# Giving up TensorE's products of constants behind the norms and around the routing positions

## The chip, the cores and the metric

The kernel runs on one core of one Trainium2 chip. The metric is device time in microseconds (us) of one execution. A core has a matrix engine (TensorE, PE in the rows; PEld is its weight load), VectorE (DVE), ScalarE (ACT), GpSimd (POOL) and SyncE (SP), which issues most DMAs. The engines run side by side and meet at semaphores; each works through its own instructions in program order.

## The reference, cut to what matters

Two layers of a transformer, for 128 context tokens (group 0) and 128 latent tokens (group 1), 1024 features, all in float32. Per layer an attention sub-layer, then a mixture of 16 experts, each behind a post-norm:

```
for l in range(2):
    hp, hs = modulate(xp, mp[0], mp[1]), modulate(xs, ms[0], ms[1])   # x * (1 + scale) + shift
    op, os_ = attention of the layer (hp / hs, caches)                # l = 0: MLA + windowed GQA, l = 1: GQA
    xp = layer_norm(ALPHA * xp + mp[2] * op, ...)                     # xs likewise
    hp, hs = modulate(xp, mp[3], mp[4]), ...
    fp, fs = moe(hp, ...), moe(hs, ...)
    xp = layer_norm(ALPHA * xp + mp[5] * fp, ...)                     # xs likewise

def moe(h, ...):
    aff = sigmoid(x @ router_w); sel = aff + router_bias              # best group of 4, best 2 experts in it
    ...
    hid = silu(x @ w_gate[e]) * (x @ w_up[e])
    y   = sum over experts of (hid * gate[e]) @ w_down[e]
```

The experts' weights are 192 MB for the two layers; with the other weights the core moves 287 MB.

## The kernel before, in words

All weights come through a ring of ten blocks of 2 MB. SP issues the loads in one fixed order; a load waits until TensorE has released the block that it overwrites. So loading runs ahead of TensorE by at most ten blocks, and stops when the ring is full.

Each engine's program is written out by hand. TensorE's runs, per layer: `modulated(l, 0)` (the normalised tokens are transposed, four 128x128 products per half of the features and group), the input projection (`project` or `project_odd`), `attention`, `ln_rows`, `modulated(l, 1)`, `route`, `experts`, `ln_rows`. In the experts the tokens are gathered by one-hot products into 64 slots per expert (`gather`), and a pair of experts takes 6 ring blocks: 4 for gate and up (`gate_up`, L1094), 2 for down (`down`, L1128). The first block of a pair is released at the fifth of the eight feature steps of `gate_up`.

A seam here is the stretch between two dense pieces of TensorE's work in which it waits for other engines. There are three kinds around the change. Letters name them below:

- Seam A, layer 0, from the attention's output projection to the experts. VectorE adds the sub-layer to x and computes the norm, group 0 first (`add_up`, `normal`, L1519), with a power on GpSimd between (L1985). TensorE transposes each group when its normalised rows are there (L739); ScalarE and VectorE copy the transposes out, modulated (L1771, L1322). Then come the router's logits (L1038, 16 columns each), `turn_back` (16 transposes of the modulated tokens, L753, copied out by ScalarE, L1757), and `route`: VectorE chooses the experts in a chain of small operations up to L1611, TensorE counts positions with products of `tri` and `ones` (L1051 to L1057), VectorE makes the first one-hots from them (L1618, L1623), and TensorE gathers (L1065). The gathered tokens are copied out by ScalarE (L1855), and `gate_up` starts.
- Seam B, from layer 0's experts to layer 1's input projection (`project_odd`, L789): norm, transposes, projection.
- Seam C, layer 1, from its attention to its experts: as A, but group 0 has been transposed and its logits computed inside the attention, so only group 1 is left.

The function `keep_busy(key, n)` (L716 to L720) issues n products of two constants, 128x128 by 128x512 in float32, into the bank that the work behind it will overwrite. A float32 product stands as two records in the trace. It is called in `modulated` before the wait for each group's normalised rows (3 then 2 products in seams A and B, 3 in C), in `route` before the wait for the chosen experts (3), and at the end of `route`, ahead of the gathers (1). No result of it is used.

Of the kernel before, what the change touches and what calls it, by code (L numbers as in the profile page):

```python
# [55 lines left out]
HALF = 512  # L56
# [247 lines left out]
def hybrid_backbone(nc, i_, o_):  # L304
# [11 lines left out]
    with ExitStack() as ctx:  # L316
        def sb(name, cols, dt=F32):
            return ctx.enter_context(nc.sbuf_tensor(name, [P, cols], dt))
# [8 lines left out]
        const = sb("const", C_COLS)  # L327
# [91 lines left out]
        def cst(c, n, rows_=P):  # L419
            return const[0:rows_, c:c + n]  # L420

        ident = cst(C_ID, P)
# [3 lines left out]
        def ar(off, n):  # L426
            return arena[:, off:off + n]

        hT = ar(0, G * D).rearrange("p (g k t) -> p g k t", g=G, k=KD)
# [75 lines left out]
        def room(eng, key, e=None):  # L505

            b, t = turn[key]
            if e is not None:
                eng.wait_ge(drained[b], e + t)
            elif t > 0:  # L510
                eng.wait_ge(drained[b], t)
# [5 lines left out]
        def fill(key):  # L517
            return filled[turn[key][0]], 1
# [4 lines left out]
        def pb(key):  # L523
            return bank[turn[key][0]]
# [142 lines left out]
        def _(pe):  # L667
# [45 lines left out]

                turn_rows(("modT", l, s), mods[l], C_SEL + 12 * s, 8)

            def keep_busy(key, n):  # L716

                room(pe, key)
                for _ in range(n):
                    nc.tensor.matmul(pb(key)[:], ident, const[:, 0:HALF], start=True, stop=True, skip_group_check=True)  # L720

            def modulated(l, s):

                for g in range(1 if (l, s) == (1, 1) else 0, G):
                    if (l, s) == (0, 0):
                        pe.wait_ge(s_x, 32)
                    else:
                        keep_busy(("hT", l, s, g, 0), 3 if (l, s) == (1, 1) else 3 - g)
                        pe.wait_ge(s_xn, G * (2 * l + s - 1) + g + 1)
                    for q in range(2):  # L730
                        rows_turned(l, s, g, q)

            def rows_turned(l, s, g, q):

                src = x if (l, s) == (0, 0) else xn_odd if (l, s) == (1, 1) else xn
                key = ("hT", l, s, g, q)
                room(pe, key)
                for k in range(4):
                    mm = nc.tensor.transpose(pb(key)[:, k * P:(k + 1) * P],  # L739
                                             src[:, g, (4 * q + k) * P:(4 * q + k + 1) * P], ident)  # L740
                    if (l, s, g, q, k) == (1, 1, 1, 0, 0):
                        mm.then_inc(*release(index[("wout", 1, 1)]))
                mm.then_inc(*fill(key))

            def turn_back(l):

                for g in range(G):
                    for q in range(2):
                        key = ("hr", l, g, q)
                        room(pe, key)  # L750
                        pe.wait_ge(*saved(("hT", l, 1, g, q)))
                        for k in range(4):
                            mm = nc.tensor.transpose(pb(key)[:, k * P:(k + 1) * P], hT[:, g, 4 * q + k, :], ident)  # L753
                        mm.then_inc(*fill(key))
# [276 lines left out]
            def logits(l, g):  # L1031
                key = ("logits", l)
                if g == 0:
                    room(pe, key)
                pe.wait_ge(*saved(("hT", l, 1, g, 0)))
                pe.wait_ge(*saved(("hT", l, 1, g, 1)))
                for k in range(KD):
                    mm = nc.tensor.matmul(pb(key)[:, g * N_EXP:(g + 1) * N_EXP], hT[:, g, k, :], rw[:, k, :],  # L1038
                                          start=(g == 0 and k == 0), stop=(k == KD - 1), skip_group_check=True)
                if g == 1:  # L1040
                    mm.then_inc(*fill(key))

            def route(l):
                for g in range(l, G):
                    logits(l, g)
                turn_back(l)
                key = ("pos", l)
                keep_busy(key, 3)
                pe.wait_ge(s_ch, l + 1)
                out = pb(key)  # L1050
                nc.tensor.matmul(out[:, 0:32], tri, chosen[:], start=True, stop=False, skip_group_check=True)  # L1051
                nc.tensor.matmul(out[:, 16:32], ones, chosen[:, 0:16], start=False, stop=True,
                                 skip_group_check=True).then_inc(*fill(key))
                room(pe, ("all", l))
                everyone = pb(("all", l))[:, 64:80]
                nc.tensor.matmul(everyone, ones, chosen[:, 0:16], start=True, stop=False, skip_group_check=True)
                nc.tensor.matmul(everyone, ones, chosen[:, 16:32], start=False, stop=True,  # L1057
                                 skip_group_check=True).then_inc(*fill(("all", l)))
                keep_busy(("xe", l, 0), 1)

            def gather(out, onehot, chunks, width):

# [200 lines left out]
            for l in range(DEPTH):  # L1263
                if l == 0:
                    pe.wait_ge(s_rows, 48)
                    pe.wait_ge(s_const, 16)
                    turn_rows(("lnT",), rows, C_ID + LN_ROW, 16)
                    pe.wait_ge(s_cwin, 1)
                    modulation(0, 0)
                    pe.wait_ge(*saved(("mod", 0, 0)))  # L1270
                    mod_columns(0, 0)
                modulated(l, 0)
                if l == 0:
                    project(0)
                    modulation(0, 1, (index[("win", 0, len(WIN[0]) - 1)],))
                else:
                    project_odd()
                attention(l)
                ln_rows(l, 0)
                modulated(l, 1)  # L1280
                if l == 0:
                    pe.wait_ge(s_load, SMALL_LOADS)
                route(l)
                experts(l)
                overflow(l)
                ln_rows(l, 1)
# [815 lines left out]
```

## Time and profile before

| | before |
|---|---|
| time, median of 3 runs | 830.72 us (828.36 to 832.08) |
| the profiled execution's own time | 832.93 us |
| its span, first to last instruction | 831.0 us |
| mean granted TensorE clock | 0.972 of full speed |
| PE busy | 760.6 us, 92% |
| DMA | 287.46 MB, mean 346 GB/s |
| products of constants (L720) | 21, in 42 records |

The span is 1.9 us shorter than the execution's own time; those 1.9 us lie before the first and after the last instruction. PE busy counts an instruction from its start to its modelled end, and consecutive ones overlap, so the start-to-start distance tells more than the mean duration. The granted clock is given as a share of 2.4 GHz: 1.00 is 2.4 GHz, 0.50 is 1.2 GHz. DMA runs at about 418 GB/s when nothing holds it back, and stands still in the seams because the ring is full.

### The profile page before, as it was taken

Reading aid. Unit: us, or ns where it says so; the run is one execution under the profiler, and the core shown is the slowest. Engines: PE = TensorE matmul, PEld = TensorE weight load, DVE = VectorE, ACT = ScalarE, POOL = GpSimd, SP = SyncE. Lnnn points to the kernel's source line nnn. Section 1 sums busy time; section 2 is a strip of 40 time slices with the busy share of each in tenths; the row PEclk is TensorE's granted clock in tenths of the full one; section 3 lists DMA queues with packets and bytes.
Section 4 is the critical chain, followed back from the end, with each engine's and each line's share of the span. In section 5 each row is a group of like instructions: output and inputs, shape, how many; then the busy total and the mean of one; then the engine's idle time right before and its main releaser. Section 6 shows DMA issues by size and latency. Waiting matters only on the chain.

```text
span 831.0 us, 9612 instructions
## 1 busy us (share of the span) xinstructions
PE 760.6 (92%) x3769; PEld 364.8 (44%) x3769; DVE 237.1 (29%) x550; ACT 150.9 (18%) x390; POOL 59.9 (7%) x116
## 2 busy tenths in 40 slices
PE   3798898999999999997899999999999999997794
PEld 1345344556544444343234564455544433443231
DVE  0004433348410101000237237475411010010056
ACT  0201212225011111111112132232211101110020
POOL 0000000000100010101000110000100001101000
PEclk9899799999999999999999999999899999999997
DMA  8999999915399999999999999752199999999971
GB/s 304 390 307 396 391 388 418 396 44 203 122 418 416 419 421 416 418 420 412 421 398 374 371 356 421 299 213 111 51 420 417 420 419 415 421 416 417 419 305 51
DMA packets 78530, 287.46 MB, mean 346 GB/s; under 512 B 6508, under 2 KB 12140, under 8 KB 62100
## 3 DMA queue, kind: packets, MB, share of 16 engines
q1 hardware_dynamic: 74452, 275.60, 83.8%
q10 hardware_dynamic: 2880, 7.03, 2.1%
q0 software_dynamic: 1152, 4.19, 1.3%
q8 instruction: 32, 0.52, 0.3%
q14 instruction: 14, 0.11, 0.0%
HBM read 278.99 MB, written 7.82 MB: 345 GB/s over the span
## 4 chain that ended last, share of the span: by engine, by line
PE 51%; SPq 29%; DMA 8%; DVE 7%; ACT 2%; issue 2%; POOL 0%; DVEq 0%; ACTq 0%
PE bank L1094 14%; SPq L600 12%; PE bank L1128 7%; SPq L595 6%; PE bank L932 5%; DMA ring<-in_exp_w_up 5%; PE bank L789 5%; SPq L596 4%; PE bank L1065 3%; DMA ring<-in_w_mod 3%; SPq L572 3%; PE bank L671 3%; PE bank L878 2%; PE bank L820 2%; ACT arena L1801 2%
## 5 line engine op out<-in xcount | busy, mean ns | idle before, releaser
L1094 PE MATMUL bank<-ring,arena 128*64 128x512 f32 x1024 | 228.5, 601 | 16.4 <-DMA ring<-in_exp_w_up 15.6
L1094 PEld LDWEIGHTS bank<-ring,arena 128*64 128x64 f32 x1024 | 75.5, 138 | 165.8 <-issue 151.5
L1128 PE MATMUL bank<-ring,arena 128*64 128x512 f32 x512 | 113.8, 595 | 5.9 <-DMA ring<-in_exp_w_down 4.9
L1678 DVE TENSOR_TENSOR arena<-bank,arena 128x256 f32<-128x256 f32 x32 | 13.6, 425 | 233.7 <-ACT arena L1847 233.7
L1128 PEld LDWEIGHTS bank<-ring,arena 128*64 128x64 f32 x512 | 36.5, 137 | 71.5 <-issue 64.3
L1065 PE MATMUL bank<-arena 128*128 128x128 f32 x512 | 62.1, 275 | 0.0
L1065 PEld LDWEIGHTS bank<-arena 128*128 128x128 f32 x512 | 59.7, 192 | 1.0 <-DVE arena L1623 0.5
L1757 ACT ACTIVATE arena<-bank 128x512 f32<-128x512 f32 (+6 forms) x67 | 37.2, 579 | 107.3 <-PE bank L789 34.0
L1847 ACT ACTIVATE arena<-bank 128x256 f32<-128x256 f32 x32 | 12.3, 384 | 227.5 <-PE bank L1094 227.5
L1694 DVE COPY arena<-bank 128x512 f32<-128x512 f32 x14 | 9.7, 691 | 118.7 <-PE bank L1128 118.7
L789 PE MATMUL bank<-ring,arena 128*128 128x256 f32 (+1 forms) x128 | 41.6, 486 | 0.0
L2004 POOL TENSOR_SCALAR arena<-const,cur 128x64 f32<-128x64 f32 x56 | 24.1, 446 | 213.3 <-PE bank L1073 210.5
L1985 POOL TENSOR_TENSOR rstd<-ss,mhalf 128x1 f32<-128x1 f32 (+2 forms) x11 | 12.6, 1142 | 360.0 <-DVE ss L1514 246.7
L820 PE MATMUL bank<-ring,cwin 128*32 128x512 f32 x256 | 32.7, 652 | 2.6 <-DMA ring<-in_w_mod 2.6
L1801 ACT ACTIVATE arena<-bank,negm 128x128 f32<-128x128 f32 (+1 forms) x64 | 26.1, 417 | 36.1 <-DVE negm L1440 36.1
L769 PE MATMUL bank<-ring,arena 128*128 128x416 f32 (+2 forms) x96 | 32.1, 495 | 0.7 <-ACT arena L1771 0.7
L789 PEld LDWEIGHTS bank<-ring,arena 128*128 128x128 f32 x128 | 24.2, 190 | 16.9 <-issue 15.3
L1859 ACT ACTIVATE arena<-bank 128x512 f32<-128x512 f32 x18 | 10.8, 597 | 108.8 <-PE bank L1128 108.8
L932 PE MATMUL bank<-ring 128*128 128x512 f32 x64 | 29.8, 599 | 0.0
L932 PE MATMUL bank<-ring,arena 128*128 128x512 f32 x64 | 29.8, 598 | 0.0
L1431 DVE TENSOR_REDUCE mx<-bank 128x2 f32<-128x512 f32 (+1 forms) x24 | 16.5, 689 | 44.0 <-PE bank L878 44.0
L692 PE MATMUL bank<-ring,cwin 128*32 128x512 f32 x128 | 18.1, 708 | 12.0 <-DMA ring<-in_w_mod 12.0
(182 smaller groups left out, 683.8 us busy)
## 6 DMA issues: line engine op xcount, KB each, us to landing
ring<-in_exp_w_gate SPq DMA_DIRECT2D x64, 1024.0 KB, 19.6
ring<-in_exp_w_up SPq DMA_DIRECT2D x64, 1024.0 KB, 20.1
ring<-in_exp_w_down SPq DMA_DIRECT2D x64, 1024.0 KB, 23.6
ring<-in_w_mod SPq DMA_DIRECT2D x24, 2048.0 KB, 19.8
expert_rows<-arena ACTq DMA_DIRECT2D x12, 512.0 KB, 7.9
ring<-in_w_out_ab SPq DMA_DIRECT2D x2, 2048.0 KB, 19.9
ring<-in_w_in_c SPq DMA_DIRECT2D x2, 2048.0 KB, 22.9
ring<-in_w_out_c SPq DMA_DIRECT2D x2, 2048.0 KB, 12.8
```

What stands on the lines that cost most here:

```text
L595: sp.dma_start(dst[:, 0], w_gate[e + t // 2, :, half]).then_inc(got(n + t)[0], 16)
L596: sp.dma_start(dst[:, 1], w_up[e + t // 2, :, half]).then_inc(got(n + t)[0], 16)
L600: sp.dma_start(dst[:, a].rearrange("p (k c) -> p k c", k=2), w_down[e + a, :, half]).then_inc(got(n + t)[0], 16)
L769: mm = nc.tensor.matmul(pb(key)[:, 0:c1 - c0], hT[:, g, k, :], w[:, k, :], start=(k == 0), stop=(k == KD - 1))
L789: mm = nc.tensor.matmul(pb(key)[:, 0:c1 - c0], hT[:, g, k, :], w[:, k, :], start=(k == 0), stop=(k == KD - 1))
L820: mm = nc.tensor.matmul(out[32 * j:32 * j + 32, :], cwin[:, k, 24 - 2 * c:56 - 2 * c], w[:, k * HALF:(k + 1) * HALF], start=(c == first an ...
L932: mm = nc.tensor.matmul(pb(key)[:], out_T(l, u)[:, ci * P:(ci + 1) * P], w[:, (c % 4) * D + hf * HALF:(c % 4) * D + (hf + 1) * HALF], star ...
L1065: mm = nc.tensor.matmul(out[:, i * width:(i + 1) * width], hr[:, g, k * P:(k + 1) * P], onehot[:, g, 0:width], start=(g == 0), stop=(g == 1))
L1094: mm = nc.tensor.matmul(pb(key)[SLOTS * hf:SLOTS * (hf + 1), :], xeT[b][:, k * P + SLOTS * a:k * P + SLOTS * (a + 1)], w[:, :, k % 4, hf * ...
L1128: mm = nc.tensor.matmul(pb(key)[SLOTS * a:SLOTS * (a + 1), :], hp[:, c:c + SLOTS], w[:, a, kf % 2, hf * HALF:(hf + 1) * HALF], start=(kf = ...
L1757: A.activation(dst, pb(key)[:] if src is None else src, ACT.Copy).then_inc(*drain(key))
L1801: ins = A.activation(prob[b][:, i * nk:(i + 1) * nk], pb(("S", l, u))[:, i * nk:(i + 1) * nk], ACT.Exp, bias=negm[b][:, i:i + 1], scale=sc ...
```

## The change

The function `keep_busy` and its four calls go. Where the call in `route` also made the bank's wait (`room`), that wait stays in its place. Nothing else moves.

```diff
-            def keep_busy(key, n):
-
-                room(pe, key)
-                for _ in range(n):
-                    nc.tensor.matmul(pb(key)[:], ident, const[:, 0:HALF], start=True, stop=True, skip_group_check=True)
-
             def modulated(l, s):
 
                 for g in range(1 if (l, s) == (1, 1) else 0, G):
                     if (l, s) == (0, 0):
                         pe.wait_ge(s_x, 32)
                     else:
-                        keep_busy(("hT", l, s, g, 0), 3 if (l, s) == (1, 1) else 3 - g)
                         pe.wait_ge(s_xn, G * (2 * l + s - 1) + g + 1)
                     for q in range(2):
                         rows_turned(l, s, g, q)
@@
                 turn_back(l)
                 key = ("pos", l)
-                keep_busy(key, 3)
+                room(pe, key)
                 pe.wait_ge(s_ch, l + 1)
                 out = pb(key)
                 nc.tensor.matmul(out[:, 0:32], tri, chosen[:], start=True, stop=False, skip_group_check=True)
@@
                 nc.tensor.matmul(everyone, ones, chosen[:, 16:32], start=False, stop=True,
                                  skip_group_check=True).then_inc(*fill(("all", l)))
-                keep_busy(("xe", l, 0), 1)
```

TensorE's program in seam A before the change, from the end of the rows of the norm's weights (L671) to the logits (L1038). An `x` behind a row is the number of such instructions in a row, a bracket what the first waits for:

```order
L671 MATMUL bank<-rows,const 128x512 [waits drained5]
L720 MATMUL bank<-const 128x512 [waits drained0]
L720 MATMUL bank<-const 128x512 x2
L739 MATMUL bank<-const,arena 128x128 [waits drained0,normalised_x_ready]
L739 MATMUL bank<-const,arena 128x128 x3
L739 MATMUL bank<-const,arena 128x128 [waits drained1]
L739 MATMUL bank<-const,arena 128x128 x3
L720 MATMUL bank<-const 128x512 [waits drained2]
L720 MATMUL bank<-const 128x512
L739 MATMUL bank<-const,arena 128x128 [waits drained2,normalised_x_ready]
```

The same place in the changed kernel, whose lines have other numbers (L739 is L732):

```order
L671 MATMUL bank<-rows,const 128x512 [waits drained5]
L732 MATMUL bank<-const,arena 128x128 [waits drained0,normalised_x_ready]
L732 MATMUL bank<-const,arena 128x128 x3
L732 MATMUL bank<-const,arena 128x128 [waits drained1]
L732 MATMUL bank<-const,arena 128x128 x3
L732 MATMUL bank<-const,arena 128x128 [waits drained2,normalised_x_ready]
```

Each group's transposes now stand directly behind the work before them, with only their wait between.

TensorE's program at the end of `route` before the change, from the last transposes of `turn_back` (L753) over the positions to the first gather (L1065):

```order
L753 MATMUL bank<-const,arena 128x128 [waits drained3,drained1]
L753 MATMUL bank<-const,arena 128x128 x3
L720 MATMUL bank<-const 128x512 [waits drained7]
L720 MATMUL bank<-const 128x512 x2
L1051 MATMUL bank<-chosen,const 128x32 [waits experts_chosen]
L1052 MATMUL bank<-chosen,const 128x16
L1056 MATMUL bank<-chosen,const 128x16 [waits drained7]
L1057 MATMUL bank<-chosen,const 128x16
L720 MATMUL bank<-const 128x512 [waits drained0]
L1065 MATMUL bank<-arena 128x128 [waits drained3,drained1,drained2,drained0,onehot_ready]
```

The same place in the changed kernel:

```order
L746 MATMUL bank<-const,arena 128x128 [waits drained3,drained1]
L746 MATMUL bank<-const,arena 128x128 x3
L1044 MATMUL bank<-chosen,const 128x32 [waits experts_chosen,drained7]
L1045 MATMUL bank<-chosen,const 128x16
L1049 MATMUL bank<-chosen,const 128x16 [waits drained7]
L1050 MATMUL bank<-chosen,const 128x16
L1057 MATMUL bank<-arena 128x128 [waits drained3,drained1,drained2,drained0,onehot_ready]
```

The positions' products now wait for the chosen experts right behind `turn_back`, and the gather for the one-hots right behind the positions. No other engine's program changes.

## Rows read from the trace of the kernel before

**Rows 1.** The page's 40 slices of the span: GB/s moved.

```profile
GB/s 304 390 307 396 391 388 418 396 44 203 122 418 416 419 421 416 418 420 412 421 398 374 371 356 421 299 213 111 51 420 417 420 419 415 421 416 417 419 305 51
```

**Rows 2.** The chain that ended last: start, duration, what.

```profile
295.49 1.30 SPq L600
...
447.77 37.83 PE bank L789 x112
```

**Rows 3.** SP's first DMA issues behind seams A and C: start, duration, count.

```profile
220.74 4.31 SPq L600 DMA_DIRECT2D ring<-in_exp_w_down  x4
...
599.30 4.32 SPq L600 DMA_DIRECT2D ring<-in_exp_w_down  x4
```

**Rows 4.** TensorE in seam A, in order of time.

```profile
193.53 2.74 PE L720 MATMUL bank<-const 128*128 128x512 f32 x6
196.10 1.04 PE L739 MATMUL bank<-const,arena 128*128 128x128 f32 x8
...
198.70 1.04 PE L739 MATMUL bank<-const,arena 128*128 128x128 f32 x8
199.88 3.72 PE L1038 MATMUL bank<-rw,arena 128*128 128x16 f32 x32
...
209.47 0.30 PE L1051 MATMUL bank<-chosen,const 128*128 128x32 f32 x2
...
211.75 3.73 PE L1065 MATMUL bank<-arena 128*128 128x128 f32 x32
```

**Rows 5.** VectorE in seam A: norms, chosen experts, first one-hots.

```profile
192.76 0.80 DVE L1519 TENSOR_SCALAR arena<-x,bnmv,rstd 128x1024 f32<-128x1024 f32 x1
...
196.71 0.81 DVE L1519 TENSOR_SCALAR arena<-x,bnmv,rstd 128x1024 f32<-128x1024 f32 x1 [0.67 <-POOL rstd L1985]
...
207.14 0.19 DVE L1611 SCALAR_TENSOR_TENSOR chosen<-chosen,gsel 128x32 f32<-128x32 f32 x1
...
210.32 0.74 DVE L1623 TENSOR_SCALAR arena<-const,pg 128x64 f32<-128x64 f32 x4
```

**Rows 6.** TensorE in seam B.

```profile
441.05 2.74 PE L720 MATMUL bank<-const 128*128 128x512 f32 x6
...
446.67 1.09 PE L739 MATMUL bank<-const,arena 128*128 128x128 f32 x8 [0.29 <-DVE arena L1519]
```

**Rows 7.** TensorE in seam C.

```profile
576.00 1.04 PE L739 MATMUL bank<-const,arena 128*128 128x128 f32 x8
578.59 2.64 PE L1038 MATMUL bank<-rw,arena 128*128 128x16 f32 x16 [1.55 <-DVE arena L1322]
581.07 3.65 PE L753 MATMUL bank<-const,arena 128*128 128x128 f32 x16
...
588.05 0.30 PE L1051 MATMUL bank<-chosen,const 128*128 128x32 f32 x2
...
590.32 3.73 PE L1065 MATMUL bank<-arena 128*128 128x128 f32 x32
```

**Rows 8.** VectorE in seam C: norm of group 1, chosen experts.

```profile
574.68 0.81 DVE L1519 TENSOR_SCALAR arena<-x,bnmv,rstd 128x1024 f32<-128x1024 f32 x1 [0.68 <-POOL rstd L1985]
...
584.71 0.19 DVE L1611 SCALAR_TENSOR_TENSOR chosen<-chosen,gsel 128x32 f32<-128x32 f32 x1
```

**Rows 9.** Stretches: us, busy PE PEld DVE ACT POOL, PEclk, DMA share, GB/s.

```profile
204.20:207.60 3.40, 3.40 (x13) 2.71 (x12) 3.00 (x16) 3.40 (x4) 0.00 (x0) 0.51 0.00 0
81.20:94.60 13.40, 10.36 (x52) 4.27 (x50) 4.24 (x13) 3.80 (x19) 0.00 (x0) 0.50 1.06 389
750.30:753.70 3.40, 3.40 (x16) 0.86 (x12) 0.00 (x0) 0.00 (x0) 0.46 (x1) 1.00 1.03 430
757.30:760.70 3.40, 3.40 (x10) 1.21 (x8) 0.00 (x0) 0.00 (x0) 0.77 (x1) 0.53 1.00 408
579.60:586.30 6.70, 6.70 (x28) 5.67 (x28) 4.92 (x20) 3.90 (x5) 0.00 (x0) 0.50 0.49 208
753.90:757.30 3.40, 1.32 (x6) 0.58 (x8) 0.85 (x2) 0.23 (x1) 2.48 (x4) 0.97 1.02 424
```

## The prediction

> **What bounds the kernel now.** I read the page's slices first. GB/s stands near 418 through both expert stretches and falls to 44, 203, 122 around seam A and to 299, 213, 111, 51 around seam C, so loading stops in the seams [rows 1]. Then the chain of waits: at 295.49 it passes to SP's issues, that is to the loads, and at 447.77 it is TensorE itself that is bound, for 37.8 us of layer 1's projection [rows 2]. Then SP's issues: behind seam A the first comes at 220.74, when the first pair of experts has released a block; behind seam C at 599.30 [rows 3]. So the experts of a layer end at a fixed distance behind the first release, and whatever moves `gate_up`'s start moves the end by as much. In seam B nothing but TensorE's own start of the projection counts. The order of TensorE, VectorE and ScalarE in each seam tells what moves that start. Last the granted clock by stretches.
>
> **What goes.** 21 products, 0.86 us each (3 products, 6 records, take 196.10 - 193.53 = 2.57 us) [rows 4]. Their 18 us of issue don't count as such: only where one is still running when the work behind it could start.
>
> **Seam A, the order alone.** Group 0's normalised rows are ready at 192.76 + 0.80 = 193.56; its transposes start at 196.10. That alone gains nothing, since group 1 is normalised only at 196.71 + 0.81 = 197.52. Group 1's transposes start at 198.70: they can start 1.15 us earlier, and with them the logits, because ScalarE's copies of group 0, 2.5 us earlier too, are no longer what they wait for. The chosen experts are ready at 207.14 + 0.19 = 207.33, but TensorE works off three products of constants and starts the positions at 209.47: 2.1 us in the way [rows 4, 5]. The one-hots are ready at 210.32 + 0.74 = 211.06, the gather starts at 211.75 behind the last product: 0.65 us [rows 4, 5]. Together 1.15 + 2.1 + 0.65 = 3.9 us at full clock.
>
> **Seam C, the order alone.** Group 1 is ready at 574.68 + 0.81 = 575.49, transposed from 576.00: 0.5. Chosen at 584.71 + 0.19 = 584.90, positions from 588.05: 3.15. One-hots to gather as in A: 0.65. Together 4.3 us [rows 7, 8].
>
> **Seam B, the order alone.** Group 1's transposes start at 446.67 and already waited 0.29 us for VectorE [rows 6]; the projection stands behind them. Nothing is gained.
>
> **What the clock takes.** The trace shows two levels. TensorE was granted 1.2 GHz from 204.2 to 207.6, although it had been busy all of the time before, with 32 logits of 16 columns each from 199.88 to 203.6 [rows 4, 9]. It was granted 1.2 GHz from 579.6 to 586.3 (a wait of 1.55 us and again logits ahead of it), from 757.3 to 760.7 (idle 2.1 of the 3.4 us ahead), and for 13.4 us from 81.2 [rows 7, 9]. At 1.2 GHz gate and up starts 10 products in 3.4 us where it starts 16 at 2.4 GHz [rows 9]; 16 transposes take 3.65 us, where 8 take 1.04 [rows 7]; a logit takes 0.165 us instead of 0.116 (3.72/32; in seam C 16 of them took 2.64, of which some 5 at full clock) [rows 4, 7]. So a 3.4 us stretch of dense work at half clock costs 1.3 to 1.7 us.
>
> The changed kernel leaves TensorE idle where products of constants stood, so I expect the fall earlier and also later than now:
>
> - A, before the logits: behind 193.6 there are 1.0 us of transposes, 2.9 us of nothing, 1.0 us of transposes, then logits. That is thinner than what stood ahead of the falls at 204.2 and 757.3, so I expect 1.2 GHz by about 198.5. Transposes at half cost 0.7, the 32 logits 1.6; between 0 and 2.3, I take 1.9. The chosen experts then come at 207.33 - 1.15 + 1.9 = 208.1, positions at once instead of at 209.47 (1.4 earlier), gather at 208.1 + 1.6 (209.47 to 211.06, as now) + 0.15 for small products at half clock = 209.85: 1.9 earlier than 211.75.
> - A, gather and first pair: all of `turn_back` is dense and may bring the clock back, but 2 us of nearly nothing follow while VectorE makes positions and one-hots. A gather at half clock takes some 7.1 us instead of 3.6. Between 0 and 3.4, one long stretch wholly at half clock; nearest are the rows of 3.4 us at half clock, 1.3 to 1.7, and I take 1.4 since part of that stretch may be over by then. Net for A: -1.9 + 1.4 = -0.5. Ends: -3.9 and +1.9.
> - B: behind 441.05 there is idle time until group 0 is ready, 1.0 us of transposes, and 2.9 us of idle up to 446.67. That is as thin as the time ahead of 757.3 [rows 6, 9], so I expect the projection to begin at 1.2 GHz. It is bound by TensorE [rows 2], so all of it counts: between 0 (the clock holds) and 3.4 (twice the 3.4 us at half), I take the single stretch, 1.5. No other work hides it.
> - C: logits and `turn_back` already ran at half clock [rows 9]; the fall a little earlier costs about 0.6 more, so chosen experts at 585.0, positions at once, gather at 586.7 instead of 590.32: 3.6 earlier. In the kernel before, the three products behind `turn_back` ran while the clock came back; now gather and `gate_up` do. Between 0 and 3.4, again 1.4. Net -2.2. Ends: -4.3 and 0.
>
> Sum: -0.5 + 1.5 - 2.2 = -1.2 us. Against the profiled execution's own 832.93 (span 831.0 and 1.9 around it) that is 831.7; that execution lies 2.2 above the median of the runs, so against 830.72 it is **829.5 us**. From the ends: -8.2 and +5.3, that is 822.5 and 836.0. The forecast is therefore no difference that can be told: a measurement of this kernel tells about 0.5%, 4.2 us.
>
> Half-clock stretches inside the expert stretches behind the first releases cost nothing before and after, since DMA sets the pace there (757.3 to 760.7 moved 408 GB/s [rows 9]). They may move about.
>
> **The rivals.**
>
> *The clock is back before both gathers.* `turn_back`'s 16 transposes may restore it and the short lull not take it. For it: at 586.3 it returned after transposes and products. Against it: the lull behind. Then A gives 1.9, C 3.6, B costs 1.5: -4.0, 826.7.
>
> *The clock never falls more than before.* Nothing but the order counts: -8.2, 822.5. Against it: the clock fell at 204.2 and 579.6 even with the products of constants, and the thin stretches are now longer [rows 9].
>
> *The clock stays at half through the dense work as well: slower.* One mechanism, in all three seams: the fall is not undone by the first dense stretch but only by a second one, as in the 13.4 us from 81.2, where TensorE was busy 10.4 us and still at 1.2 GHz [rows 9]. Then gather with `gate_up` pays 3.4 twice and the projection 3.4, and A's logits their 2.3: A +1.9, B +3.4, C 0: +5.3, 836.0. It decides when the half-clock stretches over dense work sum to more than 16 us over the three seams, against the 8.2 of gain. Against it: at 760.7 the clock was back after one stretch of gate and up [rows 9].
>
> The Trainium skill's page "TensorE: Matmul & The Clock Gate", section "HAM oscillation — how this bites in real kernels", tells of a kernel in which every group of products behind a wait for DMA starts throttled, and advises to order the work so that TensorE stays warm; by that account each of the three seams pays a throttled start, which is the forecast's time or this rival's. The trace agrees at 757.3, behind a wait for DMA, where the clock is 0.53 of 2.4 GHz [rows 9].
>
> *It doesn't matter at all*, because something else restarts the loads: 830.7. Against it: the loads move 44 GB/s in the slice from 187 us and resume with SP's issue at 220.74 [rows 1, 3].
>
> **How the numbers follow.** Forecast (-1.2, own range 826.5 to 832.5) 0.56; clock back before the gathers 0.15; clock never falls further 0.07; clock stays at half 0.13; no effect 0.09. Faster than 826.6: all of 822.5's case, nearly half of 826.7's, a little of the forecast: 0.17. Slower than 834.9: somewhat over half of the slow case and a little of the forecast: 0.10. Same: 0.73. The range that leaves out 2 in 10 runs from 825.5 to 834.0.
>
> **What would show it.** In seam A, positions start 0.05 to 0.1 us behind the chosen experts, and the gather as close behind the one-hots; logits at 0.165 us each with the clock at 0.50. Gather starts near 209.9 and 586.7 on the old scale. In B the projection begins at the same distance behind the norm, with clock 0.50 for about 3.4 us. SP's first issue of w_down in each layer moves by A's and C's net. I am wrong if the gathers run at half clock for their whole length in both layers and `gate_up` too (slower), or if the clock at all three seams is full (faster).

## The result and the profile after

| | before | after |
|---|---|---|
| time, median | 828.82 us (826.94 to 832.08, 9 runs) | 833.75 us (831.2 to 837.15, 9 runs) |
| ratio | | 1.0051 (95% interval 1.003 to 1.0071) |
| profiled execution, own time and span | 832.93, 831.0 us | 833.75, 831.9 us |
| mean granted clock in it | 0.972 | 0.967 |
| PE busy | 760.6 us | 752.8 us |

The change makes the kernel slower by 0.5%, some 4.2 us (2.5 to 5.9). The differences in us given here and below are worked out from the recorded ratio and its interval; the plain difference of the two medians is 4.9. The forecast was 1.2 us faster. Already here something asks for care: the profiled executions differ by 0.8 us only. The profile before came from an execution slower than the nine timed ones of the table. Two single executions of later runs, one without seam B's products and one with narrow products, took 1467 and 1580 us and stand in no ratio.

Where each profiled execution spent its time can be read from five distances on TensorE: from the start of the norm's weight rows (L671, eight records) of layer 0 to the first gate and up (A), on to the same rows behind layer 0's experts, from there to those of layer 1 (B, with the whole attention), on to layer 1's first gate and up (C), and on to the end.

| us | A | experts 0 | B | C | to the end |
|---|---|---|---|---|---|
| before | 26.21 | 221.40 | 132.37 | 24.80 | 236.21 |
| after | 27.49 | 221.34 | 133.70 | 23.50 | 236.50 |
| difference | +1.28 | -0.06 | +1.33 | -1.30 | +0.29 |

The sum of the differences is +1.5; the stretch up to seam A was 0.6 shorter, though nothing in it is changed, which leaves the span's +0.9. The two expert stretches differ by no more than 0.3 us between the executions, so what a seam gains or loses does reach the end in full, as the prediction had it.

TensorE in seam A after (start, duration, line, operands, count, and the wait in brackets):

```profile
189.37 3.68 PE L671 MATMUL bank<-rows,const 128*128 128x512 f32 x8
192.98 1.09 PE L732 MATMUL bank<-const,arena 128*128 128x128 f32 x8
196.94 1.55 PE L732 MATMUL bank<-const,arena 128*128 128x128 f32 x8 [2.87 <-DVE arena L1511]
198.28 6.85 PE L1031 MATMUL bank<-rw,arena 128*128 128x16 f32 x32
204.97 3.24 PE L746 MATMUL bank<-const,arena 128*128 128x128 f32 x16
208.95 0.38 PE L1044 MATMUL bank<-chosen,const 128*128 128x32 f32 x2 [0.73 <-DVE chosen L1603]
...
210.66 5.46 PE L1057 MATMUL bank<-arena 128*128 128x128 f32 x32 [0.16 <-DVE arena L1615]
...
216.86 7.52 PE L1086 MATMUL bank<-ring,arena 128*64 128x512 f32 x34
```

The queue is gone as expected: group 1's transposes follow the norm, the positions stand 0.15 us behind the chosen experts (208.80) and the gather 0.05 us behind the one-hots, where there were 2.1 and 0.65 us [rows 4, 5]. The logits are counted here by their records, two to a product, as the prediction counts them: seam A's 32 are 16 products. These 32 take 6.85 us instead of 3.72 and the gather 5.46 instead of 3.73 [rows 4]. The stretches of that execution say why (us; busy PE, PEld, DVE, ACT, POOL; granted clock; DMA share; GB/s):

```profile
197.20:207.60 10.40, 10.40 (x53) 10.40 (x52) 6.16 (x20) 3.21 (x7) 0.00 (x0) 0.51 0.37 156
...
211.20:214.20 3.00, 3.00 (x16) 3.00 (x16) 2.86 (x7) 0.07 (x1) 2.09 (x6) 0.50 0.00 0
446.80:450.00 3.20, 2.74 (x10) 2.23 (x11) 1.14 (x4) 1.66 (x5) 0.00 (x0) 0.50 1.06 388
580.00:586.60 6.60, 6.50 (x31) 6.53 (x32) 5.15 (x18) 2.16 (x4) 0.00 (x0) 0.50 0.66 277
590.00:593.20 3.20, 3.20 (x18) 3.20 (x17) 3.09 (x8) 0.60 (x1) 2.56 (x8) 0.50 0.00 0
```

In seam A TensorE is at 1.2 GHz from 197.2 to 207.6, over the second transposes, all logits and nearly all of `turn_back`, comes back to 2.4 GHz for the lull, and falls again in the gather. Before, it was at half clock from 204.2 to 207.6 alone [rows 9]. In seam C it is at half clock over the logits (3.57 us for 16) and again in the gather. Seam B, which was at full clock before, has the projection's start at half:

```profile
443.29 1.09 PE L732 MATMUL bank<-const,arena 128*128 128x128 f32 x8 [1.49 <-DVE arena L1511]
447.26 1.97 PE L732 MATMUL bank<-const,arena 128*128 128x128 f32 x8 [2.88 <-DVE arena L1511]
449.02 7.53 PE L782 MATMUL bank<-ring,arena 128*128 128x512 f32 x16
```

Behind the second group's norm the eight transposes take 1.97 us instead of 1.09 [rows 6], then the projection follows; nothing starts earlier in return. Seam C after, in order of time:

```profile
571.90 3.60 PE L671 MATMUL bank<-rows,const 128*128 128x512 f32 x8
577.46 1.09 PE L732 MATMUL bank<-const,arena 128*128 128x128 f32 x8 [1.96 <-DVE arena L1511]
580.11 3.57 PE L1031 MATMUL bank<-rw,arena 128*128 128x16 f32 x16 [1.55 <-DVE arena L1314]
583.51 3.41 PE L746 MATMUL bank<-const,arena 128*128 128x128 f32 x16
587.49 0.38 PE L1044 MATMUL bank<-chosen,const 128*128 128x32 f32 x2 [0.56 <-DVE chosen L1603]
...
589.20 5.47 PE L1057 MATMUL bank<-arena 128*128 128x128 f32 x32 [0.16 <-DVE arena L1615]
```

The gather starts 17.30 us behind the weight rows instead of 20.33, and its slower run gives 1.7 of these 3.0 us back. SP's first issue of w_down follows in both layers; in layer 0 it is at

```profile
221.39 3.80 SPq L600 DMA_DIRECT2D ring<-in_exp_w_down  x3
```

0.65 us later than in [rows 3], as A's gate and up is (216.86 against 216.22).

### The profile page after: what moved, and what is told of

It is laid out like the page before. It is cut to its first block, busy times and chain, and to the rows that moved or that the text cites. A ratio compares the mean times of both kernels' runs of the same rounds, so it can differ in the third digit from the quotient of the medians.

```text
span 831.9 us, 9530 instructions
## 1 busy us (share of the span) xinstructions
PE 752.8 (90%) x3727; PEld 365.6 (44%) x3727; DVE 237.3 (29%) x550; ACT 151.0 (18%) x390; POOL 59.9 (7%) x116
## 4 chain that ended last, share of the span: by engine, by line
PE 48%; SPq 29%; DVE 10%; DMA 8%; issue 2%; ACT 2%; POOL 0%; DVEq 0%
PE bank L1086 14%; SPq L600 12%; PE bank L1120 7%; SPq L595 6%; DMA ring<-in_exp_w_up 5%; PE bank L782 5%; PE bank L925 5%; PE bank L1057 4%; SPq L596 4%; DMA ring<-in_w_mod 3%; SPq L572 3%; PE bank L871 2%; PE bank L813 2%; ACT arena L1793 2%; PE bank L1031 1%
## 5 line engine op out<-in xcount | busy, mean ns | idle before, releaser
L1057 PE MATMUL bank<-arena 128*128 128x128 f32 x512 | 65.5, 285 | 0.3 <-DVE arena L1615 0.3
L1057 PEld LDWEIGHTS bank<-arena 128*128 128x128 f32 x512 | 62.8, 201 | 0.5 <-DVE arena L1615 0.5
```

The lines of the kernel that those rows point to most:

```text
L1057: mm = nc.tensor.matmul(out[:, i * width:(i + 1) * width], hr[:, g, k * P:(k + 1) * P], onehot[:, g, 0:width], start=(g == 0), stop=(g == 1))
```

## The experiments

Theory 1: the products bought clock. The wide products behind the norms keep TensorE at 2.4 GHz over the logits and the projection, those in `route` over the gather, and the clock is worth more than the queue. Theory 2, the rival, takes different forms: the products act only by their place in the queue, or the loss comes from the gathers alone, or the difference lies outside the seams.

**The norms' products alone taken away.**

```diff
-                        keep_busy(("hT", l, s, g, 0), 3 if (l, s) == (1, 1) else 3 - g)
```

> The products of constants behind the norms go (seams A, B and C); those in route stay. Theory 1 (what the norms' products kept up is TensorE's clock over the router's logits and over layer 1's projection): seam A gains 1.15 us by the order and loses 3.1 on 32 logits at 0.21 us each instead of 0.116 and 0.5 on transposes, B loses 1.4, C about 0.7: +4 to +5 us against the kernel before, with the clock at 0.50 over the logits of layer 0. Theory 2 (the products only stand in the way, and the loss of the changed kernel comes from the gathers behind route): the norms' part alone gives -1 to -2 us.

Measured: 837.36 against 832.4 us, ratio 1.0047 (1.0029 to 1.0066), +3.9 us. Distances: A 28.04, B 134.03, C 24.33. As theory 1 had it, if just below its +4 to +5; theory 2's -1 to -2 is out. Against the 4.2 us of the whole change, nearly all of the loss is in this part.

**Route's products alone taken away.**

```diff
-                keep_busy(key, 3)
+                room(pe, key)
...
-                keep_busy(("xe", l, 0), 1)
```

> Only the products in route go (three ahead of the positions, one ahead of the gathers, in both layers); those behind the norms stay. Theory 1: the queue in front of the positions and gathers goes, 2.1 + 0.65 us in seam A and 3.15 + 0.65 in C, and about 1.5 to 1.7 us each is given back by a gather or first gate and up at half clock: -2 to -4 us against the kernel before. Theory 2 (the loss of the changed kernel comes from here): +3 us or more, with gather and gate and up at half clock in both layers.

Measured: 831.72 against 832.4 us, ratio 0.9992 (0.9971 to 1.0013). Neither: no difference that can be told, where theory 1 said -2 to -4 and theory 2 +3 (the interval is -2.4 to +1.1 us, so only theory 1's upper edge lies inside). The stretches at half clock in this execution:

```profile
202.60:212.80 10.20, 9.52 (x44) 9.04 (x45) 8.11 (x33) 3.88 (x5) 1.89 (x5) 0.50 0.00 0
585.00:591.90 6.90, 6.67 (x32) 6.68 (x33) 6.34 (x27) 0.60 (x1) 4.01 (x11) 0.52 0.00 0
```

In seam C the gather lies inside the second of them:

```profile
584.28 0.38 PE L1051 MATMUL bank<-chosen,const 128*128 128x32 f32 x2 [1.97 <-DVE chosen L1610]
...
586.10 6.46 PE L1064 MATMUL bank<-arena 128*128 128x128 f32 x32
```

TensorE waited 1.97 us for the chosen experts, at full clock until then; the clock fell at 585.0, and the gather took 6.46 us instead of 3.73 and the positions' products 0.6 us instead of 0.4. So the queue that is saved (gather 3.7 us earlier in C) comes back as clock to more than half: C is 23.80, A 26.10.

**Seam B's products alone taken away.**

```diff
-                        keep_busy(("hT", l, s, g, 0), 3 if (l, s) == (1, 1) else 3 - g)
+                        if (l, s) != (1, 0):
+                            keep_busy(("hT", l, s, g, 0), 3 if (l, s) == (1, 1) else 3 - g)
```

> Only the five products behind the norm ahead of layer 1's projection (seam B) go. Theory 1: nothing stands earlier, and the projection's first 3.4 us run at half clock, with eight transposes: +1.3 us or up to +2.6, clock 0.50 at the projection's start. Theory 2 (the projection has slack or the clock holds): 0.

Measured: ratio 1.0026 (1.0004 to 1.0047), +2.2 us; B is 135.12. The clock fell while TensorE was idle and did not return with the first dense work:

```profile
443.80:450.40 6.60, 5.41 (x13) 3.35 (x14) 4.18 (x8) 2.39 (x7) 0.28 (x1) 0.50 1.05 385
```

Theory 1, within its +1.3 to +2.6. This execution also had a seam A with the products kept in which the clock never fell: 25.02 us, against 26.21 in the profile before, with the same code. That was the first sign that one profile does not stand for the kernel.

**Seam A's norm products alone taken away**, by the same edit with `(0, 1)`.

> Only the five products behind the norm of seam A go. Theory 1: the transposes start 1.15 us earlier, 32 logits at 0.21 us instead of 0.116 cost up to 3.1 and the transposes 0.7 at most: seam A 1 to 2.5 us longer than before, the rest as before: +1 to +2.5 us. Theory 2 (the logits are paced by their weight loads and not by the clock): -1.15.

Measured: ratio 1.0044 (1.002 to 1.0069), +3.7 us; A is 29.43, B and C 132.41 and 24.79. The logits:

```profile
197.45 6.85 PE L1039 MATMUL bank<-rw,arena 128*128 128x16 f32 x32
204.14 3.65 PE L754 MATMUL bank<-const,arena 128*128 128x128 f32 x16
207.59 3.38 PE L720 MATMUL bank<-const 128*128 128x512 f32 x6
```

The loss is above theory 1's range, though its interval (1.7 to 5.7 us) reaches into it: the three products ahead of the positions still stand there, now behind a `turn_back` that is late itself. The form of theory 2 in which the logits are paced by weight loads whatever the clock is out: 0.21 us a record at half clock, 0.116 at full. The losses measured alone, 3.7 for A and 2.2 for B, sum to more than the 3.9 of all the norms' products together; the intervals (1.7 to 5.7, 0.3 to 3.9 and 2.4 to 5.5) leave room for that.

**Every product kept in place and length, but narrow.** Each product of 512 columns becomes four of 16:

```diff
-                for _ in range(n):
-                    nc.tensor.matmul(pb(key)[:], ident, const[:, 0:HALF], start=True, stop=True, skip_group_check=True)
+                for _ in range(4 * n):
+                    nc.tensor.matmul(pb(key)[:, 0:16], ident, const[:, 0:16], start=True, stop=True, skip_group_check=True)
```

> Every product of constants is kept in place and in length, but as four products of 16 columns instead of one of 512 (about 0.9 us, as a logit takes 0.116 us per record). So TensorE's order and its waits are those of the kernel before, and what it does in the seams is what the logits do. Theory 1 (the wide products buy clock, and wide columns are what buys it): it has both costs, the queue in the way and the half clock: +6 to +10 us against before, slower than the changed kernel. Theory 2 (the products act only by their place and time): like the kernel before, within 1 us.

Measured: ratio 1.0178 (1.0138 to 1.0217), +14.8 us. TensorE from the logits of seam A to the gather, with the three former products of 512 columns now as 24 records, and below it the clock:

```profile
203.64 3.65 PE L753 MATMUL bank<-const,arena 128*128 128x128 f32 x16
207.09 5.14 PE L720 MATMUL bank<-const 128*128 128x16 f32 x24
212.06 0.61 PE L1051 MATMUL bank<-chosen,const 128*128 128x32 f32 x2
...
216.01 5.42 PE L1065 MATMUL bank<-arena 128*128 128x128 f32 x32
```

```profile
202.30:219.40 17.10, 16.75 (x80) 16.64 (x80) 9.23 (x34) 3.89 (x5) 2.09 (x6) 0.50 0.01 1
```

TensorE is busy 16.75 of 17.10 us and at half clock throughout. This is the decisive run: same order, same waits, hardly any idle time, and A 32.65, B 135.29, C 28.21. So the rival that the products act only by their place and time is out: with the narrow products TensorE was occupied and the clock was at half, while with the wide ones in the same places none of the four profiled executions of the kernel before had more than 6.8 us at half clock in one seam. The loss is more than theory 1's 6 to 10 because the narrow products slow down themselves (24 in 5.14 us; the 24 ahead of seam A's transposes, at full clock, took 2.75). How the 14.8 us divide between the two was not measured.

**The changed kernel and the kernel before, profiled again.** Both unchanged.

> The changed kernel once more, for a second profiled execution: the first had seam A at 27.49 us from the norm's weight rows to the first gate and up, B at 133.70 to the same rows of layer 1, C at 23.50, where the kernel before had 26.21, 132.37 and 24.80. Theory 1 (the clock's falls decide, and where one falls shifts from execution to execution): the stretches outside the seams repeat within 0.2 us, A lies between 26 and 29, B between 133 and 135.5, C between 22.5 and 25, with the logits of A at half clock again. Theory 2 (each part's cost is fixed): all three repeat within 0.2 us.

> The kernel before once more, for a second profiled execution. Theory 1: A between 25.0 (no fall, as in the run without B's products) and 26.2, B 132.4, C 24.8. Theory 2: A 26.2 again.

> The kernel before, a third profiled execution, to see one with a mean clock of 0.975 or more. Its timed executions go with the mean clock: 826.4 to 828.1 us at 0.979 to 0.982, 832.6 to 835.4 at 0.967. Theory 1: if this one has a clock of 0.975 or more, seams A and C together are 3 to 6 us shorter than the 51.0 of the first two, since the clock does not fall over the logits or not for long; if it has 0.967, it repeats them. Theory 2: the difference lies outside the seams.

> The kernel before, a fourth profiled execution, with the same purpose and the same expectations as the third.

| execution | own time, us | mean clock | A | B | C |
|---|---|---|---|---|---|
| before, first | 832.93 | 0.972 | 26.21 | 132.37 | 24.80 |
| before, second | 832.6 | 0.967 | 27.86 | 132.41 | 23.13 |
| before, third | 826.65 | 0.979 | 25.03 | 132.42 | 21.98 |
| before, fourth | 827.99 | 0.979 | 25.03 | 132.41 | 21.98 |
| mean of before | | | 26.0 | 132.4 | 23.0 |
| after, first | 833.75 | 0.967 | 27.49 | 133.70 | 23.50 |
| after, second | 833.29 | 0.962 | 27.18 | 134.09 | 23.42 |
| mean of after | | | 27.3 | 133.9 | 23.5 |

The expectation for the second of before missed A (27.86, where 25.0 to 26.2 was said) and C (23.13 for 24.8); the clock was at half from 202.7 to 209.5 in its seam A and from 581.6 to 585.0 in its seam C. Otherwise theory 1, with two corrections. Seams A and C together are 47.0 us in the third and the fourth, 4.0 shorter than in the first two, as was expected; but of the 6.2 us between the spans of the first and the third another 2.3 lie ahead of seam A (its weight rows start at 190.01 and 187.72), so theory 2 holds for that part. And over all its timed executions the clock orders the time less sharply than was expected (numbers in the last section). The kernel before has executions with and without the falls. In the third TensorE stays at full clock over the logits of both layers:

```profile
197.58:203.43 5.85, 5.57 (x48) 5.33 (x49) 5.57 (x19) 3.06 (x7) 0.00 (x0) 1.00 0.30 125
575.19:579.25 4.06, 3.78 (x33) 3.54 (x33) 3.83 (x12) 1.81 (x3) 0.00 (x0) 1.00 0.99 414
```

and its seam C, in order of time, is 2.8 us shorter than that of the first execution [rows 7]:

```profile
575.19 1.93 PE L1038 MATMUL bank<-rw,arena 128*128 128x16 f32 x16 [1.55 <-DVE arena L1322]
576.96 1.51 PE L753 MATMUL bank<-const,arena 128*128 128x128 f32 x12
...
579.25 2.74 PE L720 MATMUL bank<-const 128*128 128x512 f32 x6
581.83 0.30 PE L1051 MATMUL bank<-chosen,const 128*128 128x32 f32 x2
...
588.57 3.65 PE L1094 MATMUL bank<-ring,arena 128*64 128x512 f32 x16 [0.73 <-issue]
```

With the products some executions keep the clock over the logits and some don't; in neither profile without them, nor in any of the nine timed executions of the changed kernel (mean clock 0.954 to 0.972, 831.2 us the fastest), was the clock as high as before's 0.979. By the means A costs 1.3, B 1.5 and C 0.5: +3.3 us, inside the interval of the timed +4.2. The means stand on four and two executions, which is few.

**One product ahead of the positions, none ahead of the gathers; the norms' products kept.**

```diff
-                keep_busy(key, 3)
+                keep_busy(key, 1)
...
-                keep_busy(("xe", l, 0), 1)
```

> Ahead of the positions one product instead of three in both layers, none ahead of the gathers; the norms' products stay. Theory 1: TensorE is free when the chosen experts come or 0.5 us later, instead of 2.1 and 3.15 us later; the one-hots lead to the gather 0.65 us earlier. Seam A 0.6 to 1.5 us shorter than before, C 1.5 to 3 shorter, less 0 to 1.7 each for a gather at half clock: -1 to -3 us in all, better than taking all of route's products away (-0.7). Theory 2 (any wide product there delays more than it saves): equal to or slower than with none of route's products, about 0.

> The same kernel as with one product ahead of the positions and none ahead of the gathers, timed again to narrow its interval (0.9977, 0.9951 to 1.0004 the first time). Theory 1: 0.996 to 0.999 again, -1 to -3 us, seam A 24 to 26 us and C 19 to 23.5. Theory 2 (the first result was chance): 1.000 or above.

Measured: ratio 0.9977 (0.9951 to 1.0004), then 0.9949 (0.9922 to 0.9976). The first of these alone settles nothing, the second is faster than before clear of its interval; the two overlap. A is 23.96 and 25.59, C 21.02 and 22.37. In the first, C runs at full clock all through, and is 1.0 us shorter than with three products in an execution without a fall either (21.98).

**Two products there in layer 1, one in layer 0.** `keep_busy(key, 1 + l)`, the rest as above.

> As the last, but two products ahead of the positions in layer 1, where TensorE waited 1.0 us for the chosen experts with one. Theory 1: where the logits of seam C ran at half clock the second product comes 0.9 us in the way, where they ran at full clock it fits into the wait: within 1 us of one product. Theory 2 (more products always keep more clock): 1 to 2 us faster than with one.

Measured: 826.93 against 832.43 us, ratio 0.9932 (0.9908 to 0.9956), 5.7 us faster than before and the fastest of all kernels run. Its seam A, from the product ahead of the positions:

```profile
204.69 1.02 PE L720 MATMUL bank<-const 128*128 128x512 f32 x2
206.36 0.41 PE L1051 MATMUL bank<-chosen,const 128*128 128x32 f32 x2 [0.65 <-DVE chosen L1610]
...
208.11 3.84 PE L1064 MATMUL bank<-arena 128*128 128x128 f32 x32 [0.16 <-DVE arena L1622]
...
212.68 7.52 PE L1093 MATMUL bank<-ring,arena 128*64 128x512 f32 x34
```

TensorE still waits 0.65 us for the chosen experts, and the gather takes 3.84 us, at full clock. The clock was at half over most of seam C's logits (C is 23.40) and back at full for the gather. Against one product the intervals overlap, so which of the two is better stays open. These runs change two things at once, the number ahead of the positions and the one product ahead of the gathers; what each is worth was not run.

## Why the prediction was wrong

- *What bounds the seams, and that they reach the end in full*: right. Each of the two expert stretches repeats within 0.5 us over all 14 profiled executions, while A runs from 23.7 to 32.7.
- *The order alone*: right. Positions behind the chosen experts by 0.15 us, gather behind the one-hots by 0.05, second transposes behind the norm: all queue that was named is gone.
- *Seam B*: right in size. 1.5 forecast; +1.3 in the first pair of profiles, +1.5 in the means, +2.2 us when timed alone.
- *The fall in A by about 198.5*: right, at 197.2. *What the logits pay for it*: the first step that failed, a mis-sized term. The price of a logit at half clock, 0.165 us, is 2.64/16, the mean over seam C's 16 logits, although some of them ran at full clock. The rows had the right price already: these logits start at 578.59, the clock fell at 579.6 and `turn_back` starts at 581.07 [rows 7, 9], so some nine of them ran at full clock, not five, and the other seven took 1.5 us. It is 0.21 (6.85/32, and 3.40 from start to start for 16 in C). The 32 of A lose 3.1 us, not 1.6. So the chosen experts of A came 2.1 us later, against 0.75 forecast, and the gather 0.45 earlier, against 1.9 (21.29 behind the weight rows, 21.74 before).
- *The gathers' half clock*: nearly right, 1.7 us in each layer (6.20 from gather to gate and up instead of 4.47) against 1.4. The forecast lull after `turn_back`, behind which the clock is lost again in the gather, is there.
- Against the same profile these make A +1.28 where -0.5 was forecast, and C -1.30 where -2.2 was: 2.7 us together.
- *"C: logits and `turn_back` already ran at half clock"*: the second step that failed. It was true of the one execution profiled and not of the kernel: in two of four profiled executions the clock never fell in A or C. The gain was summed against an execution whose clock had already fallen in both seams. Over four executions C before averages 23.0, not 24.8, and the changed kernel's 23.5 is a loss of 0.5 where the forecast had a gain of 2.2. Together the three seams of before average 2.0 us less than in the execution the sum was made against, so this step weighs about as much as the first. Subtracting 2.2 us to get from that execution to the median moved the starting point but left the sum of gains and losses as it was, though the executions without a fall still had the clock over their logits to lose.
- *The rivals*: the slower one (half clock through a second dense stretch, 836.0) did not happen in the changed kernel's two profiles, where each gather and the projection had one such stretch. It happened in part in the projection of the run without B's products (at half until 450.4, 5.4 us behind its transposes' start), over the gather and behind it in C of the run without route's (585.0 to 591.9), and with the narrow products. The loss came by a path between forecast and rival, with the logits paying. The two faster rivals did not occur. That the clock never falls further than before was refuted by the first profile. The range, 825.5 to 834.0, held the median of 833.75, but by luck: it reaches 3.3 us above the 830.72 that it was built on, while the change cost 4.2 against a kernel before whose nine executions had a median of 828.82. The sign was wrong.
- *What the experiments split*: behind the norms the clock is worth more; in `route`, three and one are too many, and none is too few: the intervals of none (0.9971 to 1.0013) and of one or two (0.9908 to 0.9956) lie apart.

Left open: why the stretch ahead of seam A, in which nothing was changed, differs by 2.3 us between executions of the kernel before; why in some executions of one kernel the clock falls in a seam and in others not; and what C's norm products do alone, which was not run.

## What to carry to other kernels

Filler work has two prices that must be summed apart: how long it stands in front of work that is ready, and what clock the work behind it would get without it. Size it to the wait, so that it ends when the awaited result comes (here one or two products instead of three), and put it ahead of wide stretches and ahead of long runs of narrow products, over or behind which the clock fell in two of four executions here even with the filler. And before a gain of a few us is summed against one profile, look whether that execution was a lucky or an unlucky one: here seams A and C of the same kernel together differed by 4.0 us with where the clock fell, as much as the whole effect.

## What the hardware showed that I had not expected

- In the run with narrow products TensorE was busy 16.75 of 17.10 us, with transposes, products of 16 and 32 columns and the start of the gather, and the granted clock was 0.50 throughout. But narrow products also ran at full clock: in the third execution of before, the 32 logits behind the wide products ran at 1.00.
- Half the clock nearly doubles the time of one record of a logit (16 columns; two records are a product), from 0.116 to 0.21 us. The weight load ahead of each slows down with it: 333 ns on average at half clock (the changed kernel's logits in seam A), 192 ns at full (the third execution of before).
- Executions of one kernel go with their mean granted clock. Of the 59 timed executions of the kernel before for which the clock is on record, the 18 at 0.978 or more took 826.4 to 832.5 us, the 19 at 0.970 or less 832.6 to 835.4: a spread of 1%. In the four profiled ones 4.0 of the 6.2 us between slowest and fastest lie in seams A and C, where the clock fell or did not, and 2.3 us ahead of seam A.
